# A decoder step on one core: the key/value stage's eviction order, the place of x's norm, who splits the first weight tile, and when the conv cache is loaded

## The reference, cut to what matters

```
mk, mv = rms_norm(mem, g_mem) @ w_k, rms_norm(mem, g_mem) @ w_v    # both are outputs
h = rms_norm(x, g_mix)
x = x + [conv group(h); gated linear attention(h)] @ w_out         # both from h @ w_in
x = x + cross attention(rms_norm(x), mk, mv)
x = x + relu(rms_norm(x) @ w_up)^2 @ w_down
y = rms_norm(x)
```

## Time and profile before

| | us |
|---|---|
| three runs | 1462.82, 1465.18, 1465.86 |
| median | 1465.18 |
| profiled execution | 1464.26 |
| its span, first to last instruction | 1462.5 |
| PE busy in the span | 1439.4 (98%) |
| PEld, DVE, ACT, POOL busy | 1410.3, 602.1, 458.3, 377.4 |

### The profile page before, as it was taken

The page is one execution under the profiler, slowest core; times in us unless marked ns, Lnnn a source line. Parts: engine busy times, 40 slices in busy tenths (PEclk is TensorE's granted clock), DMA queues, the critical chain, the costliest instruction groups (busy, mean ns, idle before and its releaser), DMA issues.

```text
span 1462.5 us, 22505 instructions
## 1 busy us (share of the span) xinstructions
PE 1439.4 (98%) x9501; PEld 1410.3 (96%) x9501; DVE 602.1 (41%) x686; ACT 458.3 (31%) x619; POOL 377.4 (26%) x298
## 2 busy tenths in 40 slices
PE   7899999999999999999999999999999999999998
PEld 7899999999899999979999999999999999999997
DVE  5649999987533555523322111222112211122224
ACT  7522254438533433412332110222002220023224
POOL 7642232115322111102222222222222222222220
PEclk9999999999999999999999999999999999999999
DMA  9411331102432511581111111111111111111113
GB/s 350 150 39 56 54 49 32 42 30 73 152 143 87 180 44 44 204 294 58 44 44 43 58 43 44 42 57 44 43 57 35 51 43 55 45 43 43 44 43 116
DMA packets 47357, 114.06 MB, mean 78 GB/s; under 512 B 7720, under 2 KB 23352, under 8 KB 45888
## 3 DMA queue, kind: packets, MB, share of 16 engines
q1 hardware_dynamic: 47296, 113.17, 24.5%
HBM read 100.85 MB, written 12.30 MB: 77 GB/s over the span
## 4 chain that ended last, share of the span: by engine, by line
PE 95%; DVE 3%; DMA 1%; ACT 1%; issue 0%; POOL 0%; SPq 0%; DVEq 0%; ACTq 0%
PE ps L1213 59%; PE ps L1314 14%; PE ps L1608 5%; PE ps L1331 2%; PE m L1284 2%; PE ps L1642 2%; PE ps L1740 1%; PE ps L1561 1%; PE m L1521 1%; PE ps L1350 1%; DVE ps L1896 1%; PE ps L1621 1%; PE m L1436 1%; PE m L1585 1%; PE ps L1552 1%; PE m L1534 1%
## 5 line engine op out<-in xcount | busy, mean ns | idle before, releaser
L620 POOL TENSOR_TENSOR w_split<-w_raw,w_split 128x512 fp32r<-128x512 f32 x234 | 321.5, 1395 | 1044.9 <-ACT w_split L694 1044.8
L1213 PE MATMUL ps<-a_op,w_split 128*128 128x344 f32 x3168 | 499.4, 319 | 0.0
L1213 PEld LDWEIGHTS ps<-a_op,w_split 128*128 128x128 f32 x3168 | 497.8, 188 | 0.5 <-issue 0.5
L1213 PE MATMUL ps<-b_op,w_split 128*128 128x344 f32 x2304 | 362.6, 319 | 0.0
L1213 PEld LDWEIGHTS ps<-b_op,w_split 128*128 128x128 f32 x2304 | 361.7, 188 | 0.2
L1314 PE MATMUL ps<-a_op,w_split 128*128 128x344 f32 x1440 | 233.2, 321 | 0.0
L1314 PEld LDWEIGHTS ps<-a_op,w_split 128*128 128x128 f32 x1440 | 226.6, 188 | 1.7 <-issue 1.4
L694 ACT ACTIVATE w_split<-w_raw 128x1024 fp32r<-128x1024 f32 x117 | 122.9, 1051 | 258.4 <-PE ps L1213 246.0
L1896 DVE SCALAR_TENSOR_TENSOR ps<-conv_in,par,ps 128x1024 f32<-128x1024 f32 x116 | 149.7, 1291 | 3.6
L2282 DVE SCALAR_TENSOR_TENSOR tmp<-ps,rstd 128x1032 f32<-128x1032 f32 x32 | 39.5, 1233 | 215.1 <-PE ps L1213 203.2
L2292 DVE TENSOR_TENSOR x_res<-x_res,ps 128x1032 f32 x24 | 29.5, 1229 | 230.8 <-PE ps L1213 230.8
(11 more groups left out here) (254 smaller groups left out, 1104.4 us busy)
## 6 DMA issues: line engine op xcount, KB each, us to landing
w_raw<-in_wt SPq DMA_DIRECT2D x117, 512.0 KB, 3.5
cache_b<-in_cache_v SPq DMA_DIRECT2D x8, 1024.0 KB, 12.0
x_in<-in_x SPq DMA_DIRECT2D x4, 1032.0 KB, 9.0
x_spill<-x_res SPq DMA_DIRECT2D x8, 516.0 KB, 2.6
w_more<-in_wt SPq DMA_DIRECT2D x8, 512.0 KB, 7.2
cache_a<-in_cache_k SPq DMA_DIRECT2D x2, 2048.0 KB, 11.1
cache_b<-in_cache_k SPq DMA_DIRECT2D x2, 2048.0 KB, 11.7
x_res<-in_x SPq DMA_DIRECT2D x1, 3096.0 KB, 11.2
```

Of the source, the lines that this page charges most:

```text
L620: gp.tensor_tensor(split(t, slot)[:, 1, part, :], src, split(t, slot)[:, 0, part, :].bitcast(F32), ALU.subtract).then_inc(w_low_done, 1)
L1213: last = pe.matmul(ps[:, c0 // CB, 0:w], w_split[:, slot, wp, k, :], src[:, k, xp, c0:c0 + w], start=(k == 0 and j == 0), stop=(k == KT - ...
```

## The change

On DVE, `kv_evac(4)` moves ahead of the wait for `rstd_ready` and of all `x_scale`; the other evictions, `x_scale` and `x_low` are put in another order. On ACT, `norm_x` moves ahead of tile 12's high halves, and `mv_read(1)` ahead of tile 16's. The low halves of tile 0 are made by DVE, in two instructions between the low parts of `m_op`, and POOL waits for them instead. SP issues `walpha` and the conv cache behind the load of tile 13.

```diff
@@ SP
-                if t == 9:
+                if t == 13:
                     sp.dma_start(walpha[:, :], a["w_alpha"]).then_inc(w_alpha_loaded, 16)
                     sp.dma_start(conv_smp[:, :, :, :], a["conv_cache"]).then_inc(conv_cache_loaded, 16)
@@ POOL
-            lo(0, 0)
+            gp.wait_ge(w_low_done, 2)
             lo(1, 1)
@@ ACT
-            for t in range(9, 13):
+            for t in range(9, 12):
                 w_high(t, t % 2)
             norm_x()
+            w_high(12, 0)
             w_high(13, 1)
...
+            mv_read(1)
             w_high(16, 0)
-            mv_read(1)
             w_high(17, 1)
@@ DVE
+            def first_low(k0):
+                part = slice(k0, k0 + KT // 2)
+                dve.tensor_tensor(w_split[:, 0, 1, part, :], w_raw[:, 0, part, :], w_split[:, 0, 0, part, :].bitcast(F32),
+                                  ALU.subtract).then_inc(w_low_done, 1)
+
+            dve.wait_ge(w_high_done, 1)
+            first_low(0)
             for k in range(KT):
+                if k == 3:
+                    first_low(KT // 2)
                 low(m_op[:, k, 1, :], m_raw[:, k, :], ...
...
             kv_evac(3)
+            kv_evac(4)
             dve.wait_ge(rstd_ready, 2)
-            x_scale(0)
-            x_scale(1)
-            kv_evac(4)
-            x_scale(2)
-            x_scale(3)
-            x_scale(4)
+            for k in range(5):
+                x_scale(k)
             kv_evac(5)
-            x_scale(5)
-            x_scale(6)
-            x_scale(7)
+            for k in range(5, KT):
+                x_scale(k)
+            x_low(0)
+            x_low(1)
             kv_evac(6)
-            for k in range(4):
-                x_low(k)
+            x_low(2)
             kv_evac(7)
-            for k in range(4, KT):
+            for k in range(3, KT):
                 x_low(k)
```

## The result

The changed kernel takes 1456.3 us (median of 5 runs, 1456.06 to 1456.46) against 1464.12 before (5 runs, 1462.82 to 1465.86): 7.8 us less, ratio 0.9946 with a 95% interval of 0.9934 to 0.9957. The forecast was 1457.2, 8.0 us under the 1465.18 of the first three runs. The span of the profiled execution went from 1462.5 to 1454.5, by 8.0.

What follows compares the result with a forecast made beforehand. TensorE's stalls were taken to bound the key/value stage before 68 us, only work the rest. Savings of 6.1 + 1.7 + 0.3, less 0.1 for hand-overs, gave 8.0 us: 1465.18 to 1457.2, range 1455.0 to 1460.5.

Steps and rivals of the forecast that it cites:

- Evictions ahead of the wait: Behind tile 10: with `kv_evac(4)` early, transposes follow without idle time and the clock stays up; 6.1 us saved.
- The 1.7 us ahead of `first_in_tile`: Before the input projection: `kv_evac(7)` starts at 58.9, so TensorE idles 0.4 us instead of 2.1; 1.7 saved.
- Tile 0, 0.3 us: At the start: tile 0's low halves on DVE free POOL for tile 1; 0.3 us saved, range -1.7 to 1.3.
- The cut at tile 8 by POOL and x's DMA: At tile 8: low halves ready only from 33.4 cut an earlier gain to 0.2 us, unless x comes sooner.
- Norm ahead of tile 12: On ACT: Ln starts at 38.1, 1/rms is there at 41.6 and not 44.13; tile 12's split stays hidden.
- Conv cache, nothing by itself: In the DMA queue: moved in front of load 14, worth nothing; -1.3 to 0 us on that load, all hidden.
- DVE late: Rival: DVE's queue stays late through 1/rms near 44.1 or slow `x_low`; 1459.0 us, 15 in 100.
- the gain was kept behind 84 us: Rival denied here: DVE's chain in 84:340 has its own start, so the end stays at 1465 us; 3 in 100.
- tile 12 never waited for POOL: Rival denied here: tile 12's split, behind the norm, comes late and TensorE idles; 1466.8 us, 2 in 100.
- the second idle time leaves it at 1.00: Before `first_in_tile`, 65.5 to 67.67 in the kernel before: the idle time was read as leaving the granted clock at 1.00.

Runs made afterwards that it cites:

- e1: The kernel before with DVE's new order alone (`kv_evac(4)` ahead of the wait, the others as changed): 1457.45 us, ratio 0.9950.
- e5: The kernel before with 26 matmuls, results not read, between tile 10 and the first value transposes: 1464.30 us, ratio 0.9997.
- e8: The changed kernel with 26 matmuls on constants, results not read, ahead of tile 0: 1455.70 us.
- e12: The changed kernel with 20 matmuls on constants ahead of tile 0: 1455.94 us, ratio 0.9946.
- e6: The changed kernel with `norm_x` put back behind tile 12's high halves: 1457.58 us.
- e10: The changed kernel with the conv cache back behind load 9: 1456.82 us.
- e4: The kernel before with the conv cache and `walpha` issued behind load 13 alone: 1464.59 us, ratio 0.9992.
- e2: The kernel before with `norm_x` ahead of tile 12's high halves alone: 1461.59 us, ratio 0.9979.
- e3: The kernel before with tile 0's low halves on DVE alone: 1464.85 us, ratio 1.000.

## Why the prediction was right, point by point

- *Evictions ahead of the wait, 6.1 us:* right, 6.05 in the trace. e1, whose edit holds this term and the next, has both in full: no idle time behind tile 10 and 0.40 us ahead of `first_in_tile`, which starts 7.1 and not 7.8 us sooner because tile 2 came 0.7 later. The place of `kv_evac(4)` alone was not tried. e5 shows that the half clock was part of it: tile 11 alone fell from 5.21 to 3.09 with the wait for the eviction left in place.
- *The 1.7 us ahead of `first_in_tile`:* right, 1.73. DVE was free for `kv_evac(7)` at 58.12, the middle of the 56.4 to 59.8 forecast, with 0.84 us to spare before tile 15: two `x_low` took 3.87 and the third 1.73. One reason given for the middle did not hold: POOL was not idle for part of it but split tiles 15 to 17 throughout. And these tiles were sized too small, at 2.52 each: tile 15 took 3.55 us, tiles 16 and 17 together 8.01 instead of 5.04. The first half of tile 16 was still done 2.7 us before TensorE wanted it. The five `x_low` behind `kv_evac(7)` took 7.70 us instead of 6.1, and `first_in_tile` did not wait for them. The rule of the Trainium skill that the prediction cites (SBUF — State Buffer, section SBUF: two separate sides), by which one of the two blocks for a whole instruction of the other, is borne out on both sides: beside each other the longest `x_low` took 2.32 us and the longest half on POOL 2.29, against 1.22 and 1.28 for the shortest here.

```profile
51.23 3.55 POOL L620 TENSOR_TENSOR w_split_more<-w_more,w_split_more 128x512 fp32r<-128x512 f32 x2 [0.78 <-ACT w_split_more L694]
54.74 8.01 POOL L620 TENSOR_TENSOR w_split<-w_raw,w_split 128x512 fp32r<-128x512 f32 x4
```

- *Tile 0, 0.3 us:* the size came out (0.2 in the profiled execution, about 0.6 over the traces), but by luck, since the reasoning did not. DVE's part was right: m_op's low halves ended at 11.05, forecast 11.0, with 0.69 a half instead of 0.6. But I took DVE's gain of up to 1.9 us to reach tile 8 and to be cut to 0.2 by POOL's split there. It was down to 0.2 at tile 2 already (16.03 against 16.23), and tile 8 waited for nothing. TensorE set the time at the start: until about 13 us it ran at about half speed, 7 instead of 11 matmuls in a window, as in the half-clock windows of rows 3, although the granted clock reads 1.00 there; tiles 0 and 1 took 8.37 us. At full speed tile 2 could have started at about 15.1, an estimate from POOL's split of tile 1 (first half ready at about 12.3) and 2.84 for a tile; e8 and e12 get part of that, 15.38 and 15.57. Two rows and two windows of the changed kernel:

```profile
7.82 8.37 PE L1332 MATMUL ps<-m_op,w_split 128*128 128x256 f32 x48 [7.82 <-DVE m_op L1806]
...
22.11 5.86 PE L1332 MATMUL ps<-m_op,w_split 128*128 128x256 f32 x48
```

```profile
10.00:11.00 1.00, 1.00 (x7) 1.00 (x7) 1.00 (x3) 1.00 (x2) 0.00 (x0) 1.00 1.08 443
...
25.00:26.00 1.00, 1.00 (x11) 1.00 (x10) 1.00 (x2) 1.00 (x2) 1.00 (x2) 1.00 1.05 429
```

- *The cut at tile 8 by POOL and x's DMA:* right as a mechanism. It is not reached in the changed kernel, but in e6 (0.70 us) and e10 (0.98).
- *Norm ahead of tile 12:* 1/rms at 41.8, forecast 41.6. What it is worth was never stated as a term; e6 gives 1.1 us, e1 close to nothing where load 12 came early.
- *Conv cache, nothing by itself:* right for the time, by e4. For the norm it is not settled, since in e10 x_sums was as late as tile 11. In the changed kernel ACT waited 1.16 us for tile 14's load, which is issued behind the conv cache; that was hidden, as forecast.
- *The rivals:* DVE late did not happen (0.4 us of idle time as forecast); e6 brought its condition, 1/rms at 44.04, and lost 1.1 us, less than the 1.8 of the rival's price (1459.0 against 1457.2); the gain was kept behind 84 us to the last 0.1; tile 12 never waited for POOL.
- *One reading was too sure:* "the second idle time leaves it at 1.00". Of the traces with that 2.1 us gap, two of five (the kernel before and e4) passed it at 1.00 and three (e2, e3, e5) ran the first part of `first_in_tile` at 0.50, for 1.5 us more. A price for it belonged in the bounds.

## What to carry to other kernels

Where each engine takes its instructions in a fixed order, look for the one short instruction that another engine waits for and that stands behind a wait of its own; putting DVE's evictions in that order was worth 7 of 8 us. The other parts, each taken out of the changed kernel alone, showed 1.1 us (norm) and 0.9 (low halves; about 0.6 over all traces), and nothing that can be put down to the conv cache; the place of `mv_read(1)` was not tried by itself. Price idle time of TensorE with the clock that follows it, and take one passed gap in one trace as a draw, not as a rule: filling the gaps with work that nobody reads told the clock from the waits in two runs. A kernel without such gaps also repeats better (five runs of the changed kernel lay 0.4 us apart and five more 0.7, but four of e10 1.7; the runs before 3 to 4).

## What the runs showed of the hardware that was not expected

- A gap of 2.12 to 2.14 us in TensorE's work was followed by the half clock in three traces and not in two, with the same instructions right around it. The two that passed had run at half clock until about 53 us, e3 until about 50.3, e2 and e5 not at all before the gap; whether that matters is open. The scatter fits the spread of the runs before, but the other timed runs have no trace, so that this is its cause is argued, not shown.
- At the start the granted clock reads 1.00 while matmuls of 256 columns start 0.213 us apart, as they do at 0.50 in tile 11 of the kernel before; with other matmuls ahead of them the 48 of tiles 0 and 1 took 6.06 us in e8, 0.126 each.
- DVE's `x_low` and POOL's splits slowed each other, POOL as much as DVE: in the changed kernel six halves on POOL (tiles 15 to 17) took 11.6 us instead of 7.6, and eight `x_low` 13.3 instead of 9.8.
